# Output projections of two later mixers: squaring on ScalarE and the gain on VectorE as results leave PSUM

## The chip, the cores and the metric

The kernel runs on one core of a Trainium2 chip. A time is the device time of one execution in microseconds (us). The core has TensorE (matmul, with its weight load shown apart as PEld), VectorE (DVE), ScalarE (ACT), GpSimd (POOL) and SyncE (SP, which issues the transfers here). They run unsynchronized and wait for each other on semaphores. The profiler records one execution, with the clock granted to TensorE: 1.0 is 2.4 GHz, 0.5 is 1.2 GHz.

## The reference, cut to what matters

The model is a first block (a mixer and a mixture of experts) and then two layers, one "even" and one "odd". In float32, for 512 tokens of width 1024:

```python
for layer in range(2):
    nw = norm_w[layer]
    f = swiglu(rmsnorm(h, nw[0]), ...)
    h = h + 0.5 * rmsnorm(f, nw[1])
    u = rmsnorm(h, nw[2])
    m = even_mixer(u, ...) if layer % 2 == 0 else odd_mixer(u, ...)   # ends in o @ w_out
    h = h + rmsnorm(m, nw[3])
    f = swiglu(rmsnorm(h, nw[4]), ...)
    h = h + 0.5 * rmsnorm(f, nw[5])
```

`rmsnorm(m, g)` is `m / sqrt(mean(m*m) + eps) * g`, over the 1024 columns of a token. The case is about `m = o @ w_out`, `h + rmsnorm(m, nw[3])`, and the next `rmsnorm(h, nw[4])`, of each of the two layers. `w_out` has 1024 rows in the even layer and 2048 in the odd one.

## The kernel before

Tokens lie on partitions in `NT` = 4 tiles of 128. `x` (in the profile `x_tokens`) holds h for all of them. A float32 matrix is multiplied as two parts, a high one rounded to the matmul's format and a low one, the rest. `product` (L446 to L450) issues three matmuls: high by high, high by low and low by high. ScalarE writes the high part of a weight (L775, L779), VectorE the low part (L808, L812), both from a raw buffer (`weight_pieces`) that SyncE fills.

The kernel is a sequence of stages. A stage (`Stage`, `block`) gives each engine its own list of instructions in written order; nothing is reordered. At its end is a barrier: the next stage's first instructions (L55 is a jump of it) start when all engines are through. Semaphore waits inside a stage tie the lists together.

**The projection** (`project`, L569) walks over the columns of `w_out` in 4 chunks of 256 (`CHUNK_COLS`). For each chunk, TensorE forms 4 units, one for each tile of tokens, each in a PSUM bank of its own (banks 0 to 3), with 3 x 8 matmuls in the even layer and 3 x 16 in the odd one. Split weights have two buffers, the raw ones one. In `run`, ScalarE and VectorE first split chunk c+1 and then evict the units of chunk c: ScalarE copies units 1 and 3 (L746), VectorE units 0 and 2 (L748), to `m` (in the profile `even_m`, and `odd_y`, where the odd layer keeps m). SyncE had chunk 0 loaded in the stage before, so it only counts up `w_in` (L647), which releases ScalarE's first split; it loads chunk 1 when the first low part is through (L662), and at its end the two gain rows nw[3] and nw[4], spread over all partitions (L666). TensorE runs one filler call first (`keep_busy`, L2433: a matmul of constants, two instructions of 512 columns in the trace), then waits for the first splits and, by the counter from L753, for VectorE to be through with the last of them.

**The seam** (`add_normed`, L2862, which uses the class `Seam`) computes for each tile: ScalarE squares the tile of m and sums the squares into one column (L2492, an ACTIVATE and an ACTIVATION_READ_ACCUMULATOR), adds eps and takes the root (L2496); VectorE inverts it (L2558), forms `part` = m * inverse * gain (L2562) and adds it to x (L2567). Then ScalarE squares x (L2501), takes the root (L2503), VectorE inverts it (L2572), GpSimd forms x * next gain (L2634), and ScalarE (even tiles, L2509) or VectorE (odd tiles, L2578) multiplies by the inverse. TensorE turns the tile by 8 transposes (L2471), ScalarE writes the high part (L2513), VectorE the low part (L2582). Ahead of each tile's transposes stand two filler calls, and three behind the last tile. SyncE loads the first pieces of the next stage's weights meanwhile (L456). That next stage is the feed-forward part (`ffn_products`), which starts with one filler call and the splits of its first weights (L2801, L2846).

## Time and profile before

| | us |
|---|---|
| Three runs, median (lowest to highest) | 3506.04 (3501.19 to 3513.92) |
| The profiled execution, its own time | 3513.73 |
| Its span, first to last instruction | 3511.9 |
| Even projection, from TensorE's first filler to its last matmul | 1814.53 to 1862.98 |
| Even seam, to TensorE's last filler | 1862.98 to 1889.91 |
| Odd projection, likewise | 3021.57 to 3115.00 |
| Odd seam, likewise | 3115.00 to 3141.93 |

Times inside the span are counted from its start. In a timeline, a row gives start, length, engine, line, operation, output and inputs, the count of merged instructions, and in square brackets the idle time of that engine ahead of it with what ended it. Lengths of instructions in a row overlap a little, so the next start tells more than the sum of lengths. In a row of windows come the length of the stretch, then each engine's busy time and count, the granted clock, the share of DMA time and GB/s.

### The profile page before, as it was taken

To read this page: it belongs to the slowest core of one execution; us is meant where nothing else is said; L and a number is where in the kernel's file an instruction comes from. 1 tells how busy PE (TensorE), PEld (TensorE's weight loads), DVE (VectorE), ACT (ScalarE), POOL (GpSimd) and SP (SyncE) were. 2 spreads that over 40 slices of the span, in tenths; PEclk is the share of its full clock that TensorE was granted. 3 is DMA by queue.
4 is the path that set the end of the run, shared out by engine and by line. 5 is a ranking of instruction groups with operands and counts; after the bars stand their busy time and mean duration, and the time that the engine had idled before them with its cause. 6 is when DMAs were issued, how large, how long until landed. Compare 5 with 4: busy or idle time off the path is not lost. (4 is left out here: it accounts for less than half of the span.)

```text
span 3511.9 us, 45082 instructions
## 1 busy us (share of the span) xinstructions
PE 3126.3 (89%) x18490; PEld 2408.1 (69%) x18490; DVE 1266.8 (36%) x1501; ACT 990.7 (28%) x1456; POOL 356.5 (10%) x230
## 2 busy tenths in 40 slices
PE   6997658877758999998778999999999989789999
PEld 4985643322327888786776888788888865778887
DVE  3237651111123332335344332333222448443322
ACT  3116410000013221334223222322224444432222
POOL 2980000000000000100101000100000007110000
PEclk8999879999879999998889999999999999899999
DMA  6523268999973333220012332233222310313332
GB/s 226 174 87 146 64 271 358 428 427 428 428 297 84 96 98 106 72 84 16 2 57 76 97 99 100 87 96 96 96 84 84 93 53 2 108 49 96 96 99 86
DMA packets 303395, 487.06 MB, mean 139 GB/s; under 512 B 15778, under 2 KB 259965, under 8 KB 289679
## 3 DMA queue, kind: packets, MB, share of 16 engines
q1 hardware_dynamic: 298474, 467.35, 38.3%
q10 hardware_dynamic: 2468, 9.20, 0.7%
q0 software_dynamic: 2304, 8.39, 0.6%
q8 instruction: 111, 1.82, 0.2%
q14 instruction: 38, 0.30, 0.0%
HBM read 457.62 MB, written 27.28 MB: 138 GB/s over the span
## 5 line engine op out<-in xcount | busy, mean ns | idle before, releaser
L448 PE MATMUL psum_banks<-u_high,f_ffn_w_high 128*128 128x512 f32 x1408 | 549.6, 390 | 0.7 <-DVE f_ffn_w_low L2846 0.7
L449 PE MATMUL psum_banks<-u_low,f_ffn_w_high 128*128 128x512 f32 x1408 | 548.8, 390 | 0.0
L450 PE MATMUL psum_banks<-u_high,f_ffn_w_low 128*128 128x512 f32 x1408 | 548.7, 390 | 0.0
L2829 DVE TENSOR_TENSOR f_ffn_w_low<-weight_pieces,f_ffn_w_high 128x2048 fp32r<-128x2048 f32 x128 | 293.5, 2293 | 403.0 <-ACT f_ffn_w_high L2790 403.0
L2790 ACT ACTIVATE f_ffn_w_high<-weight_pieces 128x2048 fp32r<-128x2048 f32 x128 | 244.0, 1907 | 325.4 <-PE psum_banks L450 322.0
L448 PEld LDWEIGHTS psum_banks<-u_high,f_ffn_w_high 128*128 128x128 f32 x1408 | 264.8, 188 | 58.6 <-issue 3.9
L450 PEld LDWEIGHTS psum_banks<-u_high,f_ffn_w_low 128*128 128x128 f32 x1408 | 264.7, 188 | 54.9
L449 PEld LDWEIGHTS psum_banks<-u_low,f_ffn_w_high 128*128 128x128 f32 x1408 | 264.7, 188 | 54.9 <-issue 0.3
L448 PE MATMUL psum_banks<-f_ffn_w_high,f_hidden_high 128*128 128x512 f32 x704 | 275.0, 391 | 3.6 <-issue 3.6
L450 PE MATMUL psum_banks<-f_ffn_w_high,f_hidden_low 128*128 128x512 f32 x704 | 274.3, 390 | 0.0
L449 PE MATMUL psum_banks<-f_ffn_w_low,f_hidden_high 128*128 128x512 f32 x704 | 274.3, 390 | 0.0
L2022 PE MATMUL psum_banks<-expert_ring,experts_x_t 128*64 128x512 f32 x1024 | 229.1, 603 | 22.9 <-DMA expert_ring<-in_expert_w_up 21.5
L2834 DVE TENSOR_TENSOR f_ffn_whole<-f_ffn_silu,psum_banks 128x512 f32<-128x512 f32 x88 | 60.5, 688 | 468.9 <-PE psum_banks L450 468.9
L2797 ACT ACTIVATE f_hidden_high<-f_ffn_whole 128x512 f32 (+1 forms) x88 | 55.6, 632 | 502.1 <-DVE f_ffn_whole L2834 502.1
L2022 PEld LDWEIGHTS psum_banks<-expert_ring,experts_x_t 128*64 128x64 f32 x1024 | 77.1, 139 | 171.9 <-issue 170.1
L448 PEld LDWEIGHTS psum_banks<-f_ffn_w_high,f_hidden_high 128*128 128x128 f32 x704 | 132.2, 188 | 32.1 <-issue 5.2
L450 PEld LDWEIGHTS psum_banks<-f_ffn_w_high,f_hidden_low 128*128 128x128 f32 x704 | 132.2, 188 | 27.4
L449 PEld LDWEIGHTS psum_banks<-f_ffn_w_low,f_hidden_high 128*128 128x128 f32 x704 | 132.3, 188 | 27.2
L2059 PE MATMUL psum_banks<-expert_ring,experts_hidden_t 128*64 128x512 f32 x512 | 128.3, 659 | 18.5 <-DVE experts_hidden_t L2089 18.5
L2634 POOL TENSOR_TENSOR weight_pieces<-x_tokens,f_ffn_whole 128x1024 f32<-128x1024 f32 x12 | 28.7, 2392 | 1129.0 <-DVE x_tokens L2567 1129.0
L2105 ACT ACTIVATE experts_silu<-psum_banks 128x512 f32<-128x512 f32 x16 | 9.6, 597 | 455.3 <-PE psum_banks L2022 455.3
L448 PE MATMUL psum_banks<-mix_in_w_high,h_t_high 128*128 128x256 f32 x416 | 117.7, 283 | 1.5 <-DVEq L753 1.3
(654 smaller groups left out, 5587.2 us busy)
## 6 DMA issues: line engine op xcount, KB each, us to landing
expert_ring<-in_expert_w_gate SPq DMA_DIRECT2D x32, 2048.0 KB, 34.8
expert_ring<-in_expert_w_up SPq DMA_DIRECT2D x30, 2048.0 KB, 35.2
expert_ring<-in_expert_w_down SPq DMA_DIRECT2D x28, 2048.0 KB, 39.6
weight_pieces<-in_ffn_w_gate SPq DMA_DIRECT2D x88, 512.0 KB, 4.0
weight_pieces<-in_ffn_w_up SPq DMA_DIRECT2D x88, 512.0 KB, 5.3
weight_pieces<-in_ffn_w_down SPq DMA_DIRECT2D x88, 512.0 KB, 4.1
weight_pieces<-in_odd_w_in SPq DMA_DIRECT2D x20, 1024.0 KB, 5.4
mix_in_mod_w<-in_w_ada SPq DMA_DIRECT2D x32, 512.0 KB, 3.7
```

The lines of the kernel that those rows point to most:

```text
L448: nc.tensor.matmul(out, lhs.high, rhs.high, start=start, stop=False, skip_group_check=True)
L449: nc.tensor.matmul(out, lhs.high, rhs.low, start=False, stop=False, skip_group_check=True)
L450: return nc.tensor.matmul(out, lhs.low, rhs.high, start=False, stop=stop, skip_group_check=True)
L2022: last = nc.tensor.matmul(k.ps[half, bank, :], self.xt[:, q, half], self.rows_of(n, a, q * HID, HID), start=q == 0, stop=q == KD - 1)
L2059: last = nc.tensor.matmul(k.ps[half, 5 + b, :], self.ht[:, c, half], self.rows_of(n, a, c * D + b * BANK, BANK), start=c == 0, stop=c == H ...
L2105: nc.scalar.activation(self.sg[:], k.ps[:, 2, :], ACT.Silu).then_inc(self.silu_ok, 1)
L2634: nc.gpsimd.tensor_tensor(self.xn[:, t % 2, :], self.k.x[:, t, :], self.next_gain, ALU.mult).then_inc(self.xg_ok, 1)
L2790: nc.scalar.activation(w.high[:, j], raw[:, j], ACT.Copy).then_inc(w_high, 1)
L2797: nc.scalar.activation(tile_of(hidden.high, t), whole[:, j, :], ACT.Copy).then_inc(h_high, 1)
L2829: nc.vector.tensor_tensor(w.low[:, j], raw[:, j], w.high[:, j].bitcast(F32), ALU.subtract).then_inc(w_low, 1)
L2834: nc.vector.tensor_tensor(whole[:, j, :], sg[:, j, :], k.ps[:, 2 * j + 1, :], ALU.mult).then_inc(whole_ok, 1)
```

## The change

Both output projections get a new kind of part, `Gained`. ScalarE squares every unit of a chunk out of PSUM, with its sum into one column per tile and chunk; VectorE then multiplies every unit out of PSUM by the slice of the gain row nw[3] into `m`. So `m` holds m * gain, and the sums of squares of m are there when the projection ends: 4 per tile. SyncE issues the load of the row nw[3] as the stage's first transfer, ahead of the count that releases ScalarE; VectorE waits for it at its products. The row nw[4] is loaded at the end as before.

`add_normed` no longer uses `Seam`. One reduction adds the 4 sums of all tiles, one root and one reciprocal serve all of them, and one three-operand instruction per tile forms x = m * inverse + x. The squares of x stay with ScalarE; the second scaling, x * inverse * next gain, is one three-operand instruction on VectorE. GpSimd has nothing left there. TensorE waits for the first square of x, runs three filler calls, then all four tiles' transposes, then three filler calls. The even projection's padding `apart` is 128 in place of 192; with the new small buffers, its split weights start 2048 bytes further on. In the odd layer the new buffers lie in unused parts of old ones.

The diff, cut to its core:

```diff
+class Gained:
+    def __init__(self, gain, gain_row, junk, sums):
+        self.gain, self.gain_row, self.junk, self.sums = gain, gain_row, junk, sums
@@ project: SyncE
+            if measured:
+                sp.dma_start(measured.gain, measured.gain_row).then_inc(gain_in, 16)
             for part in walk:
@@ project: copies, on ScalarE and on VectorE
+                        elif part.gained:
+                            convolve(part, c, u)
@@ project: ScalarE
+            def square(c, u):
+                eng.wait_ge(mm, c * NT + (u + 2))
+                eng.wait_ge(squared, c * NT + (u + 1))
+                nc.scalar.activation(measured.junk[:, u % 2, :], k.ps[:, u, 0:CHUNK_COLS], ACT.Square, scale=D ** -0.5,
+                                     accum_out=measured.sums[:, u, bass.ds(c, 1)]).then_inc(squared, 1)
@@ project: VectorE
+            def multiply(part, c, u):
+                v.wait_ge(gain_in, 16)
+                v.wait_ge(squared, c * NT + (u + 3))
+                nc.vector.tensor_tensor(part.dest(c, part.units[u]), k.ps[:, u, 0:CHUNK_COLS],
+                                        part.gained.gain[:, bass.ds(c * CHUNK_COLS, CHUNK_COLS)], ALU.mult).then_inc(free_v, 1)
@@ add_normed: TensorE
-            seam.tensor(pe)
+            pe.wait_ge(squares, 1)
+            keep_busy(k, 0, 3)
+            for t in range(NT):
+                pe.wait_ge(xn_ok, t + 1)
+                for i in range(KD):
+                    last = nc.tensor.transpose(banks(t)[:, i, :], xn[:, t % 2, i * P:(i + 1) * P], k.c("ident"))
+                last.then_inc(turned, 1)
+            pe.wait_ge(low_ok, 1)
+            keep_busy(k, 0, 3)
@@ add_normed: ScalarE
-            seam.scalar(eng)
+            eng.wait_ge(summed, 1)
+            nc.scalar.activation(f_moments, f_moments, ACT.Sqrt, bias=eps[:, 0:1]).then_inc(f_roots, 1)
+            measure(0)
+            measure(1)
+            measure(2)
+            high(0)
+            measure(3)
+            high(1)
+            high(2)
+            high(3)
@@ add_normed: VectorE
-            seam.vector(v)
+            nc.vector.tensor_reduce(f_moments, sums, AX.X, ALU.add).then_inc(summed, 1)
+            v.wait_ge(f_roots, 1)
+            nc.vector.reciprocal(f_moments, f_moments).then_inc(f_inverse, 1)
+            v.wait_ge(f_inverse, 1)
+            def add(t):
+                nc.vector.scalar_tensor_tensor(out=x[:, t, :], in0=f[:, t, :], scalar=f_moments[:, t:t + 1], in1=x[:, t, :],
+                                               op0=ALU.mult, op1=ALU.add).then_inc(x_ok, 1)
+            def normed(t):
+                v.wait_ge(roots, t + 1)
+                nc.vector.reciprocal(moment(t), moment(t)).then_inc(inverse, 1)
+                v.wait_ge(inverse, t + 1)
+                if t >= 2:
+                    v.wait_ge(turned, t - 1)
+                nc.vector.scalar_tensor_tensor(out=xn[:, t % 2, :], in0=x[:, t, :], scalar=moment(t), in1=next_gain,
+                                               op0=ALU.mult, op1=ALU.mult).then_inc(xn_ok, 1)
@@ even_layer (odd_layer likewise)
+        project(k, "even_out", mix_t, a["even_w_out_2"][0], [
+            (0, D, token_units(NT), by_tokens(m), Gained(gains[:, 0, :], everywhere(nw[3:4]), junk, m_sums))], out_raw,
+                also=[(gains[:, 1, :], everywhere(nw[4:5]))], apart=128)
```

VectorE's order in the seam is `add` of tiles 0, 1 and 2, `normed(0)`, `add(3)`, `normed(1)`, `normed(2)`, `low(0)`, `normed(3)`, `low(1)` to `low(3)`.

VectorE in the even seam, before; `even_m` is the projection's result, `even_post_part` the scaled tile, `even_post_xn` the tile for the transposes:

```order
L2558 RECIPROCAL even_post_stats<-even_post_stats 128x1
L2562 SCALAR_TENSOR_TENSOR even_post_part<-even_m,even_post_stats,even_post_gains 128x1024
L2567 TENSOR_TENSOR x_tokens<-x_tokens,even_post_part 128x1024
L2558 RECIPROCAL even_post_stats<-even_post_stats 128x1
L2562 SCALAR_TENSOR_TENSOR even_post_part<-even_m,even_post_stats,even_post_gains 128x1024
L2572 RECIPROCAL even_post_stats<-even_post_stats 128x1
L2567 TENSOR_TENSOR x_tokens<-x_tokens,even_post_part 128x1024
L2558 RECIPROCAL even_post_stats<-even_post_stats 128x1
L2562 SCALAR_TENSOR_TENSOR even_post_part<-even_m,even_post_stats,even_post_gains 128x1024
L2572 RECIPROCAL even_post_stats<-even_post_stats 128x1
L2567 TENSOR_TENSOR x_tokens<-x_tokens,even_post_part 128x1024
L2578 TENSOR_SCALAR even_post_xn<-even_post_xn,even_post_stats 128x1024
```

VectorE in the even seam, now:

```order
L2960 TENSOR_REDUCE even_post_stats<-even_m_sums 128x4
L2962 RECIPROCAL even_post_stats<-even_post_stats 128x4
L2966 SCALAR_TENSOR_TENSOR x_tokens<-even_m,even_post_stats,x_tokens 128x1024 x3
L2971 RECIPROCAL even_post_stats<-even_post_stats 128x1
L2975 SCALAR_TENSOR_TENSOR even_post_xn<-x_tokens,even_post_stats,even_post_gains 128x1024
L2966 SCALAR_TENSOR_TENSOR x_tokens<-even_m,even_post_stats,x_tokens 128x1024
L2971 RECIPROCAL even_post_stats<-even_post_stats 128x1
L2975 SCALAR_TENSOR_TENSOR even_post_xn<-x_tokens,even_post_stats,even_post_gains 128x1024
L2971 RECIPROCAL even_post_stats<-even_post_stats 128x1
L2975 SCALAR_TENSOR_TENSOR even_post_xn<-x_tokens,even_post_stats,even_post_gains 128x1024
L2980 TENSOR_TENSOR u_low<-psum_banks,u_high 128x8x128
L2971 RECIPROCAL even_post_stats<-even_post_stats 128x1
```

Two long operations per tile (a three-operand product and an addition) became one, the reciprocals of the first norm became one, and the product with the next gain came over from GpSimd.

TensorE around the even seam, before (L2433 are filler calls, two recorded instructions each; L2471 are transposes):

```order
L2874 UNCONDITIONAL_BRANCH
L2433 MATMUL psum_banks<-const_table 128x512 x2
L2471 MATMUL psum_banks<-const_table,even_post_xn 128x128 x8
L2433 MATMUL psum_banks<-const_table 128x512 x2
L2471 MATMUL psum_banks<-const_table,even_post_xn 128x128 x8
L2433 MATMUL psum_banks<-const_table 128x512 x2
L2471 MATMUL psum_banks<-const_table,even_post_xn 128x128 x8
L2433 MATMUL psum_banks<-const_table 128x512 x2
L2471 MATMUL psum_banks<-const_table,even_post_xn 128x128 x8
L2433 MATMUL psum_banks<-const_table 128x512 x3
L55 UNCONDITIONAL_BRANCH
```

TensorE there, now (L2466 are the filler calls, L2928 the transposes, L2744 the next stage):

```order
L55 UNCONDITIONAL_BRANCH
L2921 UNCONDITIONAL_BRANCH
L2466 MATMUL psum_banks<-const_table 128x512 x3
L2928 MATMUL psum_banks<-const_table,even_post_xn 128x128 x32
L2466 MATMUL psum_banks<-const_table 128x512 x3
L55 UNCONDITIONAL_BRANCH
L2744 UNCONDITIONAL_BRANCH
L2466 MATMUL psum_banks<-const_table 128x512
```

The fillers between the tiles are gone; three calls stand ahead of all transposes and three behind them.

## Rows read from the trace of the kernel before

**Rows 1.** The page: busy time, share of the span and instructions of each engine.

```profile
PE 3126.3 (89%) x18490; PEld 2408.1 (69%) x18490; DVE 1266.8 (36%) x1501; ACT 990.7 (28%) x1456; POOL 356.5 (10%) x230
```

**Rows 2.** Timeline, TensorE, even seam: start us, us, engine line, op, count, idle before.

```profile
1866.83 3.39 PE L2433 MATMUL psum_banks<-const_table 128*128 128x512 f32 x4 [3.85 <-DVE even_post_part L2562]
...
1886.25 1.09 PE L2471 MATMUL psum_banks<-const_table,even_post_xn 128*128 128x128 f32 x8 [0.52 <-DVE even_post_xn L2578]
...
1887.17 2.74 PE L2433 MATMUL psum_banks<-const_table 128*128 128x512 f32 x6
```

**Rows 3.** The same, odd seam.

```profile
3118.84 3.68 PE L2433 MATMUL psum_banks<-const_table 128*128 128x512 f32 x4 [3.84 <-DVE odd_post_part L2562]
...
3139.19 2.74 PE L2433 MATMUL psum_banks<-const_table 128*128 128x512 f32 x6
```

**Rows 4.** Timeline, ScalarE, even seam.

```profile
1863.02 0.38 ACT L746 ACTIVATE even_m<-psum_banks 128x256 f32<-128x256 f32 x1 [5.27 <-PE psum_banks L450]
...
1863.68 0.20 ACT L2486 ACTIVATE even_post_stats<-const_table 128x1 f32<-128x1 f32 x1 [0.29 <-PEq L55]
...
1864.96 0.29 ACT L2496 ACTIVATE even_post_stats<-even_post_stats,const_table 128x1 f32<-128x1 f32 x1
...
1868.06 1.06 ACT L2501 ACTIVATE even_post_junk<-x_tokens 128x1024 f32<-128x1024 f32 x1 [1.45 <-DVE x_tokens L2567]
...
1869.03 0.19 ACT L2501 ACTIVATION_READ_ACCUMULATOR even_post_junk<-x_tokens 128x1 f32 x1
...
1879.00 1.00 ACT L2513 ACTIVATE u_high<-psum_banks 128x1024 fp32r<-128x1024 f32 x1
```

**Rows 5.** Timeline, VectorE, even seam.

```profile
1865.48 1.28 DVE L2562 SCALAR_TENSOR_TENSOR even_post_part<-even_m,even_post_stats,even_post_gains 128x1024 f32<-128x1024 f32 x1
...
1868.14 3.41 DVE L2562 SCALAR_TENSOR_TENSOR even_post_part<-even_m,even_post_stats,even_post_gains 128x1024 f32<-128x1024 f32 x1
...
1888.43 1.23 DVE L2582 TENSOR_TENSOR u_low<-psum_banks,u_high 128x1024 fp32r<-128x1024 f32 x1 [1.11 <-ACT u_high L2513]
```

**Rows 6.** Timeline, GpSimd, even seam.

```profile
1868.11 2.36 POOL L2634 TENSOR_TENSOR even_post_xn<-x_tokens,even_post_gains 128x1024 f32<-128x1024 f32 x1 [117.45 <-DVE x_tokens L2567]
```

**Rows 7.** Transfers issued at L666: ns min/median/max, then landing of all of them.

```profile
L666 SPq DMA_DIRECT2D even_post_gains<-in_norm_w x2: 418/421/424, 1837.8 to 1838.3; - x2
...
DMA to landing us min/median/max: 4.1/5.9/9.0
```

**Rows 8.** Timeline, start of the even projection and its first chunks, three engines.

```profile
1814.36 2.19 ACT L775 ACTIVATE even_out_w_high<-weight_pieces 128x512 fp32r<-128x512 f32 x4 [1.03 <-SPq L647]
...
1814.53 2.04 PE L2433 MATMUL psum_banks<-const_table 128*128 128x512 f32 x2 [3.84 <-PEq L55]
...
1816.67 0.58 PE L448 MATMUL psum_banks<-even_out_w_high,even_mix_t_high 128*128 128x256 f32 x1
...
1824.89 2.29 DVE L812 TENSOR_TENSOR even_out_w_low<-weight_pieces,even_out_w_high 128x2048 fp32r<-128x2048 f32 x1 [7.37 <-ACT even_out_w_high L779]
...
1829.10 0.38 ACT L746 ACTIVATE even_m<-psum_banks 128x256 f32<-128x256 f32 x1 [3.97 <-PE psum_banks L450]
...
1837.58 0.42 DVE L748 COPY even_m<-psum_banks 128x256 f32<-128x256 f32 x1 [0.18 <-PE psum_banks L450]
```

**Rows 9.** Windows: length, busy us and counts (PE, PEld, DVE, ACT, POOL), clock, DMA.

```profile
1816.60:1818.30 1.70, 1.63 (x7) 1.63 (x8) 0.92 (x2) 0.00 (x0) 0.00 (x0) 0.50 0.01 5
...
1818.60:1862.90 44.30, 44.30 (x377) 44.17 (x376) 9.91 (x11) 8.32 (x10) 0.00 (x0) 1.00 0.29 96
...
3025.40:3030.00 4.60, 4.58 (x21) 4.58 (x22) 1.73 (x2) 0.00 (x0) 0.00 (x0) 0.50 0.35 100
...
3030.50:3114.90 84.40, 84.40 (x746) 84.30 (x744) 16.31 (x11) 13.37 (x10) 0.00 (x0) 1.00 0.24 80
...
3127.40:3132.60 5.20, 5.18 (x13) 3.01 (x14) 5.16 (x6) 3.66 (x7) 2.81 (x1) 0.50 0.00 0
...
1890.00:1900.00 10.00, 9.40 (x39) 7.22 (x40) 4.79 (x5) 5.88 (x7) 0.00 (x0) 1.00 0.58 149
```

77 lines of the change are left out of this document (60 added, 17 removed).

## The prediction

> **What bounds the kernel now.** The page comes first: TensorE is busy for 89% of the span, VectorE for 36%, ScalarE for 28% [rows 1]. So work on the other engines counts only where TensorE stands idle for it. The next view is TensorE in order of time around the two places that the diff touches. While an output projection runs, its matmuls are back to back and the evictions lie beside them. The stage behind it (from here the seam) is different: from 1862.98 (the first filler's start 1866.83, less the 3.85 us idle ahead of it), where the last projection matmul ends, to 1889.91 (1887.17 + 2.74), where the last filler ends, TensorE runs 32 short transposes and some fillers and waits for the other engines [rows 2]. That is 26.93 us. The odd seam has nearly the same length: 3115.00 (3118.84 - 3.84) to 3141.93 [rows 3]. These two stretches, 54 us of 3512, are all that the change can shorten. Everything behind them is TensorE's own work, so a gain there is kept.
>
> Then the engines inside the even seam. ScalarE squares each tile of the projection's result before VectorE may scale it; the first scaled product starts at 1865.48 [rows 5]. VectorE then runs for each tile a three-operand product and an addition. The first product takes 1.28 us, the second 3.41 [rows 5]. The second starts at 1868.14, GpSimd's product of the same stage at 1868.11, and GpSimd's lasts until 1870.47 [rows 6]; 1.08 us later VectorE's ends. GpSimd has four such products, and VectorE three long ones beside them. I read the 2.1 us of excess as waiting for GpSimd.
>
> The Trainium skill ("SBUF — State Buffer", section "SBUF: two separate sides") says that a VectorE instruction with two SBUF inputs and a GpSimd one that reads SBUF take a shared port pair in turns, whole instruction by whole instruction. By that rule every product costs 1.28 us once GpSimd is out of the seam; were it wrong, the sum would be that of the fourth case below. The trace agrees, with the 1.08 us just named.
>
> **Step 1, the projection.** ScalarE now squares all four results of a chunk and VectorE multiplies all four, where each copied two. Two more squares (0.38 us as the copy [rows 4], and 0.19 us to read the accumulator, as behind the square of x) and two more products (0.42 us as the copy [rows 8]) lie beside 11.3 us of matmuls per chunk. What TensorE needs from VectorE is the low half of the next weights: for chunk 1 it ends at 1827.18 (1824.89 + 2.29), and the last result of chunk 0 is evicted only at 1829.10 [rows 8], so 1.9 us are to spare. I cost the loop at nothing; without that cover it would be 1 us per chunk. The gain row's transfer, 512 KB, is issued first. Its wait stands at VectorE's first product, some 13 us later, with the three other products and the next low half queued behind it, and TensorE behind those. The row's landing has no exact match: transfers issued at the same line landed after 4.1 to 9.0 us [rows 7]. It is hidden.
>
> What is not hidden is its issue. ScalarE's first weight split is released by SyncE [rows 8], which must now issue the row first: 0.42 us, the median of the even gains' two issues [rows 7]. TensorE's start hangs on that split, so 0.42 us are lost per projection. In the even one a second loss is possible: the filler ended at 1816.57 and the first matmul followed at 1816.67 [rows 8]; now 0.5 us are idle between them. The granted clock stood at 0.50 until 1818.3, 1.7 us after that start, and at 1.00 behind it. In the odd one, with 1.8 us idle there, it stood at 0.50 for 4.6 us after the start [rows 9]. If the longer pause sets the clock's rise back likewise, 2.9 us more run at half clock, 1.4 us lost. Between 0 and 1.4 I take 0.5, since a pause of 0.5 lies nearer to the short one.
>
> **Step 2, the tail.** Before, the last copy ended 0.42 us after the last matmul and ScalarE's next stage began at 0.70 [rows 4]. Now the last result goes through square, accumulator and product in a row: 0.38 + 0.19 + 0.42, with hops about 1.0; plus the same 0.28 for the barrier gives 1.3.
>
> **Step 3, the first row sum.** Gone are four squares of the result and the long products with the gain. In their place is one reduction over 128x16, for which no row stands: between a 128x1 operation of 0.16 and a copy of 256 columns of 0.42, I take 0.2, nearer to the small one. From the start of the square root to the scaled product was 0.52 (1864.96 to 1865.48 [rows 4, 5]). So the first addition begins at 1.3 + 0.2 + 0.05 + 0.52, about 2.05 after the last matmul, and ends at 3.35 (1.28, as above). The square of x with its accumulator takes 1.16 (1868.06 to 1869.22 [rows 4]): at **4.6** TensorE may begin its fillers.
>
> **Step 4, the fillers.** Three calls make six instructions, ahead of all transposes. TensorE is at the lower of its two clock levels (1.2 GHz) then: after 3.8 us idle, the four filler instructions of before took 3.39 us, and 3.68 in the odd seam [rows 2, 3]. At full clock (2.4 GHz) six take 2.74 [rows 2], so four 1.8. Six at the low level are 3.68 x 6/4, at most 5.5. In the even seam the clock rose before the fourth ended (3.39 is less than 3.68), some 3 us after the start; in the odd one it stayed at 0.50 through 5.2 us of work from 3127.4 on [rows 9]. With the rise at 3 us, 3.3 instructions are done and 2.7 at 0.46 are left: 4.3. So 4.3 to 5.5; I take 4.9, the middle. The first transposes can begin at **9.5**. The scaled row is ready by 7.2, so these fillers are what is late.
>
> **Step 5, the rest.** From there in a chain: transposes of tile 0, 1.05; their high half 1.0; the square of tile 3, which ScalarE runs behind it, with its root 1.5; reciprocal and hop 0.3; product 1.28; transposes 1.1; fillers 2.74 at full clock: 8.9, less small overlaps **8.8**. VectorE's last low half ends within 0.3 us of that. The seam becomes 18.3 us (17.7 to 18.8).
>
> **The sum.** 26.9 - 18.3 - 0.42 = 8.2 us per seam, 16.4 for both, less 0.5: 15.9. The profiled execution took 3513.73 us (span 3511.9 and 1.8 around it); it becomes 3497.8. The median of the runs shown is 7.7 lower, 3506.04, with 12.7 between the ends of the three, so I forecast **3490**.
>
> **Rivals.**
> 1. *The clock falls before the seam ends.* TensorE idles 1.6 us ahead of the last transposes. If that is enough, the last six fillers take 5.5 instead of 2.74: 2.7 per seam, 3495.4. For: the projection's start in step 1. Against: once at full clock it stayed there over a pause of 0.52 us ahead of the old seam's last transposes [rows 2], and at 1.00 from 1890 to 1900, with 0.6 us idle [rows 9]. Neither is as long as 1.6.
> 2. *The clock is still full at the fillers.* Then six take 2.74 and each seam is 2.2 shorter: 3485.7. Against it speak the slow fillers after a shorter pause, 3.8 us [rows 2, 3].
> 3. *A hidden loss in the projection.* The gain row's packets delay chunk 1's weights, or the moved weight buffers change the spacing of matmuls. The even projection's recorded matmuls are 44.30 / 377 = 0.1175 us apart, the odd one's 84.40 / 746 = 0.1131, 4% less [rows 9]; 4% of both projections' 139 us is 5.6. With little for the weights: some 6 us, 3496.
> 4. *The three-operand products stay slow by themselves.* This one ends slower. The new seam has eight of them on VectorE in a row. If 3.3 us is their price when operands lie so, GpSimd or not, VectorE needs 2.05 + 8 x 3.3 + four low halves of 1.23 + reciprocals 0.8 = 34.2 us, 7.7 more per seam than 26.9 with the late start, 3521. It decides from 2.4 us per product. Against: the first, with GpSimd idle, took 1.28 [rows 5].
> 5. *The row is late.* VectorE stands at its first product, and TensorE at chunk 1. That costs only beyond about 15 us after issue; the longest landing was 9.0 [rows 7].
>
> **Chances.** Forecast within 3 us: 0.62. Rival 1: 0.14. Rival 2: 0.08. Rival 3: 0.10. Rival 4: 0.03, rival 5: 0.01; 0.02 is for something else. A measurement of this kernel tells about 0.3%, 10.5 us, from no change. Forecast, rival 2 and a half of rivals 1 and 3 are beyond it, 0.82; the other halves are within, 0.13; with rivals 4 and 5 and the medians' own spread slower has 0.05. The range takes in rivals 1 to 3 and a few us for the medians: 3481 to 3500.
>
> **What would show it.** The seam from last projection matmul to last filler: 17.7 to 18.8 us. Three-operand products at 1.28, GpSimd empty there. Fillers starting 4.6 after the last matmul and lasting 4.3 to 5.5. The first projection matmul 0.4 later against the stage's start. TensorE's spacing within the projection unchanged. I am wrong if the fillers don't delay the transposes, if VectorE's products exceed 1.3, or if TensorE waits inside the projection.

## The result

| | us |
|---|---|
| The changed kernel, five runs, median (lowest to highest) | 3488.13 (3486.49 to 3489.62) |
| The kernel before, five runs beside it | 3506.33 (3501.19 to 3513.92) |
| Ratio, with its 95% interval | 0.9946 (0.9936 to 0.9957) |
| The profiled execution of the changed kernel | 3489.62, span 3487.8 |
| Even seam / odd seam (before: 26.93 each) | 18.41 / 18.84 |
| First filler of the projection to the next stage's filler, even / odd | 67.02 / 112.72 (before: 75.83 / 120.81) |

The median fell by 18.2 us, 0.52%, and 3490 had been forecast. Here are the rows of the changed kernel that answer to those of before. First the page's line of the engines; against [rows 1], GpSimd has 8 instructions and 19 us less, the four products of either seam.

```profile
PE 3117.5 (89%) x18470; PEld 2398.9 (69%) x18470; DVE 1256.5 (36%) x1509; ACT 984.8 (28%) x1478; POOL 337.5 (10%) x222
```

The timeline of TensorE, even seam, then odd, answers to [rows 2, 3]. The last projection matmul ends at 1857.46 (1862.09 - 4.63) and at 3099.01.

```profile
1862.09 5.24 PE L2466 MATMUL psum_banks<-const_table 128*128 128x512 f32 x6 [4.63 <-ACT even_post_junk L2941]
1867.16 1.91 PE L2928 MATMUL psum_banks<-const_table,even_post_xn 128*128 128x128 f32 x16
...
1872.19 1.09 PE L2928 MATMUL psum_banks<-const_table,even_post_xn 128*128 128x128 f32 x8 [1.45 <-DVE even_post_xn L2975]
1873.12 2.74 PE L2466 MATMUL psum_banks<-const_table 128*128 128x512 f32 x6
...
3103.62 5.49 PE L2466 MATMUL psum_banks<-const_table 128*128 128x512 f32 x6 [4.61 <-ACT odd_post_junk L2941]
...
3115.11 2.74 PE L2466 MATMUL psum_banks<-const_table 128*128 128x512 f32 x6
```

ScalarE and then VectorE in the even seam, answering to [rows 4, 5]: the last result is squared (L799) and multiplied (L851) in a row, the barrier lies between 1858.4 and 1858.8, the three additions (L2966) are one merged row of 3.68 us, and the scaled rows (L2975) take 1.28 each. VectorE stands still once, for 1.01 us, for transposes of TensorE.

```profile
1857.49 0.38 ACT L799 ACTIVATE even_m_junk<-psum_banks 128x256 f32<-128x256 f32 x1 [2.25 <-PE psum_banks L450]
...
1858.79 0.20 ACT L2935 ACTIVATE even_post_stats<-const_table 128x1 f32<-128x1 f32 x1 [0.83 <-PEq L55]
1860.88 1.06 ACT L2941 ACTIVATE even_post_junk<-x_tokens 128x1024 f32<-128x1024 f32 x1 [1.56 <-DVE x_tokens L2966]
```

```profile
1858.06 0.42 DVE L851 TENSOR_TENSOR even_m<-psum_banks,even_post_gains 128x256 f32<-128x256 f32 x1 [2.30 <-ACT even_m_junk L799]
1858.82 0.17 DVE L2960 TENSOR_REDUCE even_post_stats<-even_m_sums 128x4 f32<-128x16 f32 x1 [0.33 <-PEq L55]
1859.57 3.68 DVE L2966 SCALAR_TENSOR_TENSOR x_tokens<-even_m,even_post_stats,x_tokens 128x1024 f32<-128x1024 f32 x3
1863.35 1.28 DVE L2975 SCALAR_TENSOR_TENSOR even_post_xn<-x_tokens,even_post_stats,even_post_gains 128x1024 f32<-128x1024 f32 x1
...
1868.31 1.28 DVE L2975 SCALAR_TENSOR_TENSOR even_post_xn<-x_tokens,even_post_stats,even_post_gains 128x1024 f32<-128x1024 f32 x1 [1.01 <-PE psum_banks L2928]
...
1872.06 3.55 DVE L2980 TENSOR_TENSOR u_low<-psum_banks,u_high 128x1024 fp32r<-128x1024 f32 x3
```

The start of the even projection, answering to [rows 8]: SyncE issues the row (L655), ScalarE's first split has waited 1.43 us where it was 1.03, and TensorE pauses 0.49 us between filler and first matmul where it was 0.1. While chunk 0 is evicted, VectorE's low half of chunk 1 ends at 1822.34 and its last product at 1825.85; TensorE has no wait there.

```profile
1809.09 0.35 SPq L655 DMA_DIRECT2D even_post_gains<-in_norm_w  x1
```

```profile
1809.52 0.63 ACT L790 ACTIVATE even_out_w_high<-weight_pieces 128x512 fp32r<-128x512 f32 x1 [1.43 <-SPq L660]
```

```profile
1809.29 2.05 PE L2466 MATMUL psum_banks<-const_table 128*128 128x512 f32 x2 [3.83 <-PEq L55]
1811.83 0.58 PE L448 MATMUL psum_banks<-even_out_w_high,even_mix_t_high 128*128 128x256 f32 x1 [0.49 <-DVEq L768]
```

```profile
1820.05 2.29 DVE L837 TENSOR_TENSOR even_out_w_low<-weight_pieces,even_out_w_high 128x2048 fp32r<-128x2048 f32 x1 [7.37 <-ACT even_out_w_high L794]
...
1825.43 0.42 DVE L851 TENSOR_TENSOR even_m<-psum_banks,even_post_gains 128x256 f32<-128x256 f32 x1 [2.09 <-ACT even_m_junk L799]
```

Windows, with the columns of [rows 9]: the even seam's fillers and what follows, the odd seam's fillers, and both projections at full clock. The matmuls come 39.40 / 349 = 0.1129 us apart in the even projection (0.1175 before) and 82.90 / 733 = 0.1131 in the odd (as before). A window also counts matmuls that its ends cut, so these quotients are slightly small, in all traces alike: from start to start it is 0.1134 in both projections here.

```profile
1862.10:1867.30 5.20, 5.20 (x8) 2.21 (x9) 5.13 (x7) 2.93 (x7) 0.00 (x0) 0.53 1.17 279
1867.30:1876.00 8.70, 6.54 (x39) 4.27 (x37) 7.26 (x7) 5.20 (x7) 0.00 (x0) 1.00 0.00 1
3103.50:3108.50 5.00, 4.88 (x6) 2.08 (x7) 4.93 (x7) 3.02 (x8) 0.00 (x0) 0.50 1.20 292
...
3016.00:3098.90 82.90, 82.90 (x733) 82.81 (x731) 19.18 (x18) 17.57 (x33) 0.00 (x0) 1.00 0.22 71
1818.00:1857.40 39.40, 39.40 (x349) 39.25 (x347) 12.67 (x18) 12.42 (x33) 0.00 (x0) 1.00 0.20 67
```

The two stretches from a projection's first filler to the next stage's filler give 8.81 + 8.09 = 16.9 us. The two profiled spans differ by 24.1. The other 7 us lie in stages that the change doesn't touch, most of them in two: from the first to the last matmul on `mix_in_w`, the first block's input weights, it took 182.5 us before and 178.7 now, and on `odd_in_w`, the odd layer's, 239.7 and 236.9. From the lists of before and of after, the first of three kinds of the former, its matmuls shorter in the mean:

```profile
L448 PE MATMUL psum_banks<-mix_in_w_high,h_t_high 128*128 128x256 f32 x416 | 117.7, 283 | 1.5 <-DVEq L753 1.3
```

```profile
L448 PE MATMUL psum_banks<-mix_in_w_high,h_t_high 128*128 128x256 f32 x416 | 116.1, 279 | 1.7 <-DVEq L768 1.4 <-DVE tok L763 0.2
```

So two profiled runs cannot be subtracted to a few us; the argument below goes by the stretches and the medians.

### The profile page after: what moved, and what is told of

Same layout as the page of the kernel before. It is cut to its first block and busy times, and to the rows that moved or that the text cites. A ratio compares the mean times of both kernels' runs of the same rounds, so it can differ in the third digit from the quotient of the medians.

```text
span 3487.8 us, 45099 instructions
## 1 busy us (share of the span) xinstructions
PE 3117.5 (89%) x18470; PEld 2398.9 (69%) x18470; DVE 1256.5 (36%) x1509; ACT 984.8 (28%) x1478; POOL 337.5 (10%) x222
## 5 line engine op out<-in xcount | busy, mean ns | idle before, releaser
L2092 PE MATMUL psum_banks<-expert_ring,experts_hidden_t 128*64 128x512 f32 x512 | 137.4, 698 | 17.7 <-DVE experts_hidden_t L2122 17.7
```

The costliest lines, as they stand in the source:

```text
L2092: last = nc.tensor.matmul(k.ps[half, 5 + b, :], self.ht[:, c, half], self.rows_of(n, a, c * D + b * BANK, BANK), start=c == 0, stop=c == H ...
```

## Experiments

All against the changed kernel. "Seam" is, as in the prediction, last projection matmul to end of the last filler. "Both stretches" is the sum of the two stretches just named (before: 196.6). The ratios are each to the kernel before on the same chip.

| kernel | median us (runs) | ratio, 95% interval | seam even / odd | both stretches |
|---|---|---|---|---|
| changed kernel | 3488.13 (5) | 0.9946 (0.9936 to 0.9957) | 18.41 / 18.84 | 179.7 |
| e1, row later | 3488.59 (4) | 0.9951 (0.9935 to 0.9968) | 17.71 / 18.89 | 177.5 |
| e2, no first fillers | 3487.92 (4) | 0.9945 (0.9929 to 0.9962) | 17.42 / 17.57 | 181.2 |
| e3, early fillers | 3487.21 (4) | 0.9950 (0.9933 to 0.9967) | 17.41 / 17.40 | 177.0 |
| e4, GpSimd beside | 3505.52 (1) | | 25.84 / 26.59 | 197.0 |
| e5, projection undone | 3499.97 (10) | 0.9979 (0.9969 to 0.9988) | 23.44 / 25.76 | 190.2 |
| e6, GpSimd's product back | 3505.33 (1) | | 24.68 / 25.78 | 192.5 |
| e7, e1 and e3 together | 3490.39 (4) | 0.9957 (0.9942 to 0.9973) | 17.41 / 19.08 | 179.9 |
| e8, fused | 3482.22 (5) | 0.9931 (0.9918 to 0.9945) | 13.69 / 14.28 | 178.6 |
| e9, fused, kept busy | 3487.65 (5) | 0.9949 (0.9935 to 0.9962) | 12.71 / 12.40 | 173.6 |
| e10, changed kernel again | 3490.13 (5) | 0.9956 (0.9943 to 0.9970) | 18.18 / 18.88 | 182.4 |
| e11, e9 with weights in place | 3480.32 (5) | 0.9925 (0.9911 to 0.9938) | 12.86 / 12.39 | 170.9 |
| e12, weights 64 bytes on | 3496.89 (8) | 0.9972 (0.9961 to 0.9982) | 18.68 / 17.70 | 185.7 |

### Is it GpSimd? (e4, e5, e6)

e4 adds GpSimd's products where they had been; nothing reads them.

```diff
+        @block.gpsimd
+        def _(pool):
+            for t in range(NT):
+                pool.wait_ge(x_ok, t + 1)
...
+                nc.gpsimd.tensor_tensor(beside[:], x[:, t, :], next_gain, ALU.mult).then_inc(beside_ok, 1)
```

> Edit of the changed kernel: GpSimd forms x * next gain into a buffer of its own that nobody reads, behind each of the four additions of a seam, as extra work. Theory (a VectorE product with two SBUF inputs and a GpSimd one take turns): of the eight three-operand products of a seam, those that meet one of the four GpSimd products take 3.3 us instead of 1.28, at least three of them; tile 0's scaled copy is ready at 11 to 13.5 us behind the last matmul instead of 7.2, and the seam grows by 3 to 6 us from 18.4. Rival (the 3.4 us of before came from the operands' place or the PSUM traffic of the time): all eight stay at 1.28, the seam at 18.4.

The seams grew by 7.4 and 7.7 us, more than expected and nearly all that the change had gained. VectorE's timeline, then GpSimd's, in the even seam: the three additions take 5.83 instead of 3.68 and the next products 3.24 to 3.45, while GpSimd works. Once it is through, at 1876.8, they are back at 1.28.

```profile
1861.76 5.83 DVE L2967 SCALAR_TENSOR_TENSOR x_tokens<-even_m,even_post_stats,x_tokens 128x1024 f32<-128x1024 f32 x3
1867.69 3.24 DVE L2976 SCALAR_TENSOR_TENSOR even_post_xn<-x_tokens,even_post_stats,even_post_gains 128x1024 f32<-128x1024 f32 x1
1870.86 3.43 DVE L2967 SCALAR_TENSOR_TENSOR x_tokens<-even_m,even_post_stats,x_tokens 128x1024 f32<-128x1024 f32 x1
1874.40 3.45 DVE L2976 SCALAR_TENSOR_TENSOR even_post_xn<-x_tokens,even_post_stats,even_post_gains 128x1024 f32<-128x1024 f32 x1
1877.95 1.28 DVE L2976 SCALAR_TENSOR_TENSOR even_post_xn<-x_tokens,even_post_stats,even_post_gains 128x1024 f32<-128x1024 f32 x1
```

```profile
1863.12 10.08 POOL L3002 TENSOR_TENSOR even_post_beside<-x_tokens,even_post_gains 128x1024 f32<-128x1024 f32 x3 [117.49 <-DVE x_tokens L2967]
1874.37 2.40 POOL L3002 TENSOR_TENSOR even_post_beside<-x_tokens,even_post_gains 128x1024 f32<-128x1024 f32 x1 [1.17 <-DVE x_tokens L2967]
```

Both engines pay: three of GpSimd's products take 10.08 us together, 3.4 each. The last starts 0.03 us ahead of VectorE's at 1874.40, takes 2.40, and VectorE ends 1.08 us behind it. The same instructions at the same lines cost 1.28 or 3.4 by what GpSimd does. So a price of their own (rival 4) is out.

e5 does the other half: GpSimd stays out, and the projections store as before, so that the norm of the result is back in the seam.

```diff
-            (0, D, token_units(NT), by_tokens(m), Gained(gains[:, 0, :], everywhere(nw[3:4]), junk, m_sums))], out_raw,
+        project(k, "even_out", mix_t, a["even_w_out_2"][0], [(0, D, token_units(NT), by_tokens(m))], out_raw,
...
+                nc.vector.scalar_tensor_tensor(out=part[:], in0=f[:, t, :], scalar=mom, in1=gain,
+                                               op0=ALU.mult, op1=ALU.mult).then_inc(product_ok, 1)
+                v.wait_ge(product_ok, t + 1)
+                nc.vector.tensor_tensor(x[:, t, :], x[:, t, :], part[:], ALU.add).then_inc(x_ok, 1)
```

> The projections store their results as the kernel before does (plain copies by both engines, no gain, no squares), and the seam does the whole of the branch's norm; GpSimd has no work in it. Per tile ScalarE squares the result, VectorE forms result times inverse times gain (1.28 us), adds it (about 1.2) and forms the scaled row (1.28). Theory (GpSimd's presence is most of the price, the moved work the rest): VectorE's row is twelve operations of 1.2 to 1.3 and four subtractions of 1.17, 19.5 us with the reciprocals, behind a start of 2.5 to 3 and with a wait or two: seam 22.5 to 24, so of the 8.5 us per seam between 26.9 and 18.4 some 4 belong to GpSimd and some 4.5 to the moved products; total 8 to 11 us above the changed kernel, and no row issue at the projection's start (first matmul 0.4 us earlier). Rival A (the moved work is all that counts, VectorE's operations are as long as before): seam near 27. Rival B (GpSimd's presence is all that counts): seam below 20.

The even seam, 23.44, lies in the expected 22.5 to 24. VectorE's product starts 2.51 us after the last matmul (1855.87), at 1.28, the addition at 1.22. The odd one, 25.76, doesn't: there TensorE's clock fell before the end, seen in its timeline by transposes of 1.97 and six fillers of 4.23 in place of 1.09 and 2.74. VectorE itself was through at 3126.56, 24.06 after the last matmul.

```profile
1858.38 1.28 DVE L2973 SCALAR_TENSOR_TENSOR even_post_part<-even_m,even_post_stats,even_post_gains 128x1024 f32<-128x1024 f32 x1
```

```profile
3122.27 1.97 PE L2928 MATMUL psum_banks<-const_table,odd_post_xn 128*128 128x128 f32 x8 [0.95 <-DVE odd_post_xn L2984]
3124.03 4.23 PE L2466 MATMUL psum_banks<-const_table 128*128 128x512 f32 x6
```

e6 keeps the projections of the changed kernel and gives GpSimd the product x * next gain again; VectorE only applies the inverse.

```diff
-                nc.vector.scalar_tensor_tensor(out=xn[:, t % 2, :], in0=x[:, t, :], scalar=moment(t), in1=next_gain,
-                                               op0=ALU.mult, op1=ALU.mult).then_inc(xn_ok, 1)
+                v.wait_ge(xg_ok, t + 1)
+                nc.vector.tensor_scalar(xn[:, t % 2, :], xn[:, t % 2, :], moment(t), None, ALU.mult).then_inc(xn_ok, 1)
...
+                nc.gpsimd.tensor_tensor(xn[:, t % 2, :], x[:, t, :], next_gain, ALU.mult).then_inc(xg_ok, 1)
```

> The changed kernel's projections and its fused addition stay; only the scaled row is split again as in the kernel before: GpSimd forms x times the next gain (about 2.4 us), VectorE applies the inverse to the product (an operation with one tensor operand). Theory (every three-operand product of VectorE beside a GpSimd product is late by about 2 us): the additions of tiles 1 to 3 run beside GpSimd's and take 3.2 to 3.5 each instead of 1.28, the operations with one tensor operand stay below 1 us; seam 20 to 23 us against 18.4, total 4 to 9 us above the changed kernel. Rival (GpSimd's product is harmless where its reader is not behind it, VectorE even saves 0.5 us per tile by the shorter operation): seam 16.5 to 18.5.

24.68 and 25.78, above even the theory's 20 to 23. The missing part is in VectorE's rows: the scaling with one tensor operand, which I had put below 1 us, took 2.65 and 2.91 beside GpSimd, and 0.75 alone. Another 1.76 us is a wait of VectorE for GpSimd's fourth product, which my own wait for a free buffer had held back.

```profile
1861.95 5.77 DVE L2967 SCALAR_TENSOR_TENSOR x_tokens<-even_m,even_post_stats,x_tokens 128x1024 f32<-128x1024 f32 x3
1867.84 2.65 DVE L2975 TENSOR_SCALAR even_post_xn<-even_post_xn,even_post_stats 128x1024 f32<-128x1024 f32 x1
...
1871.79 2.91 DVE L2975 TENSOR_SCALAR even_post_xn<-even_post_xn,even_post_stats 128x1024 f32<-128x1024 f32 x1
...
1874.81 0.75 DVE L2975 TENSOR_SCALAR even_post_xn<-even_post_xn,even_post_stats 128x1024 f32<-128x1024 f32 x1
```

The Trainium skill ("SBUF — State Buffer", section "SBUF: two separate sides") names two kinds of VectorE instruction that lock out GpSimd and are locked out by it: those with two SBUF inputs, and those in a two-port performance mode. The 0.75 us alone and 2.65 beside GpSimd agree with the second kind; that this operation runs in such a mode is my reading, since no row tells the mode.

What follows from the three: in the even seam, taking GpSimd out without the move gives 26.93 - 23.44 = 3.5 us, moving the products into the projection with GpSimd's product left in 26.93 - 24.68 = 2.3, and both 8.5. These are not pure shares: e5 and e6 also have the new order of TensorE, without fillers between the tiles, and e6 has the wait of 1.76 us just named, which the kernel before has not. The two halves help each other: the move leaves VectorE with operations in an unbroken row, and each one that a GpSimd product meets is late. In the whole, e5 is 12 us above the changed kernel's median, and e4 and e6, a single run each, 17; for e6, 4 to 9 had been expected.

### What comes behind the fillers? (e2, e3)

e2 takes the three filler calls ahead of the transposes out.

```diff
-            pe.wait_ge(squares, 1)
-            keep_busy(k, 0, 3)
```

> Edit of the changed kernel: the three filler calls ahead of the seam's first transposes are left out. Theory (they hold the transposes back, 9.7 us behind the last matmul where the scaled tile is ready at 7.2, but they also raise the clock for what follows): transposes of tile 0 start at 7.2 and take 1.9 at half clock, the six filler instructions at the end take 5.5 instead of 2.74, and the seam comes out at 19 to 21 us, against 18.4; the total is 1 to 5 us above the changed kernel's. Rival (the clock is not worth its fillers, since the transposes are few): the seam is 15.8 to 17 us and the total 3 to 5 us below.

e3 starts six of them at once instead.

```diff
-            pe.wait_ge(squares, 1)
-            keep_busy(k, 0, 3)
+            keep_busy(k, 0, 6)
```

> Edit of the changed kernel: six filler calls (twelve instructions) run at once from the seam's start, without a wait for the first square of x, in place of three behind that square. Theory (a pause of 1.3 us leaves the clock at its full level, as the 1.45 us ahead of the last transposes did): fillers from 1.3 to 6.8 us behind the last matmul, at full clock, transposes of tile 0 at 7.2 instead of 9.7, seam 15.9 us; 2.5 us per seam and 5 in all below the changed kernel. Rival (the clock falls in the pause at the barrier): twelve instructions at 0.9 us end at 12.2, the seam is 21 us and the total 5 us above.

Both seams end at 17.4 to 17.6, 1.0 to 1.4 below the changed kernel's, by opposite ways. None of the four lengths that had been expected came true (19 to 21 or 15.8 to 17 for e2, 15.9 or 21 for e3), and the medians differ by less than the runs spread. Without fillers (first fence) the transposes of tile 0 run at the lower level, 1.97 us, but start 7.24 us after the last matmul. With early ones (second fence) TensorE pauses only 1.36 us, keeps full clock over it, and the transposes start at 7.23. In both, VectorE's row decides.

```profile
1863.13 1.97 PE L2926 MATMUL psum_banks<-const_table,even_post_xn 128*128 128x128 f32 x8 [7.24 <-DVE even_post_xn L2973]
```

```profile
1856.44 5.39 PE L2466 MATMUL psum_banks<-const_table 128*128 128x512 f32 x12 [1.36 <-PEq L55]
1862.32 1.09 PE L2927 MATMUL psum_banks<-const_table,even_post_xn 128*128 128x128 f32 x8 [0.49 <-DVE even_post_xn L2974]
```

In e3's odd seam the clock did fall for a while: behind a pause of 1.50 us the transposes of tiles 1 and 2 took 3.36 us together, with the granted clock at 0.50 from 3104.3 to 3106.5. The last transposes were back at 1.09, and the seam lost nothing by it.

```profile
3103.01 3.36 PE L2927 MATMUL psum_banks<-const_table,odd_post_xn 128*128 128x128 f32 x16 [1.50 <-DVE odd_post_xn L2974]
```

From its first addition (2.11 us after the last matmul) VectorE has 8 operations at 1.2 start to start, 4 low parts at 1.15 and 4 reciprocals at 0.19 without a break: 2.1 + 9.6 + 4.6 + 0.8 = 17.1. That is the seam's second bound, 1.3 behind the first. It was named in the prediction ("within 0.3 us of that") but as an end that coincides, not as what remains when the fillers go.

### The start of the projection (e1, e7)

e1 issues the row behind the first weights' count.

```diff
             for part in walk:
...
                 if loaded and not part.chunks:
                     sp.sem_inc(w_in, 16)
...
+                if measured:
+                    sp.dma_start(measured.gain, measured.gain_row).then_inc(gain_in, 16)
```

> Edit of the changed kernel: SyncE first counts up for ScalarE's first weight split and then issues the gain row's transfer. Theory (the issue stands on the path to TensorE's start, and the longer pause behind the first filler sets the clock's rise back in the even projection): from filler start to first matmul 2.14 us in the even projection (now 2.54) and 3.85 in the odd (now 4.22), and half clock for 1.7 us behind the even start instead of 3.9; 1.8 us less in all, all of it ahead of the seams, which stay at 18.4 and 18.8. Rival (the slow start has another cause than the pause): only 0.4 per projection comes back, 0.8 in all, and half clock lasts 3.9 us as before. Second rival (VectorE now waits for the row): TensorE has a pause at chunk 1.

```profile
1811.90 2.04 PE L2466 MATMUL psum_banks<-const_table 128*128 128x512 f32 x2 [3.84 <-PEq L55]
1814.11 0.58 PE L448 MATMUL psum_banks<-even_out_w_high,even_mix_t_high 128*128 128x256 f32 x1 [0.17 <-DVEq L768]
```

From filler to first matmul 2.21 us instead of 2.54 in the even projection, 3.92 instead of 4.22 in the odd; the issue costs 0.3, once for each. The clock rose 4.0 us after the filler's start, as before the change (4.0), against 6.5 in the changed kernel. (The even seam of 17.71 is no doing of the edit: its first six fillers took 4.54 us, where the same six took 5.24 in the changed kernel's profile, 5.02 in e10 and 5.49 in e12.) Over all traces of this study the even projections with a pause of 0.46 to 0.50 us rose after 5.6 to 7.6 us (eight traces, mean 6.4), those with 0.1 to 0.34 after 3.8 to 6.6 (six traces: 3.8, 4.0, 4.0, 4.3, 6.0, 6.6, mean 4.8). So the longer pause goes with 1.6 us more at half clock on average, 0.8 us of work; single runs of the two groups overlap. The odd projections show no such thing: there the clock rose 8.0 to 8.8 us after the filler's start with 1.8 or 1.9 us of pause (four traces) and 7.7 to 8.9 with 2.2 to 3.1 (ten traces). The total, 3488.59, can't show so little.

e7 is e1 and e3 together.

> Both small gains together: the gain's row issued behind the first weights' count, and the seam's first fillers not waiting for the first tile's squares (six of them at once). Theory: the projection's first matmul 0.3 us and the rise of the clock 2.5 us earlier in the even one (about 1.3 us of work), seam 17.4 instead of 18.4 and 18.8: 1.3 to 2.5 us per segment, 3 to 5 us in total, median 3483 to 3486. Rival (VectorE takes all of it back): within 1.5 us of the changed kernel.

The forecast of 3483 to 3486 was wrong: 3490.39. The even seam came out as said, 17.41, but the even projection's clock rose 5.9 us after the filler's start, not about 4. In the odd seam the clock fell before the last transposes, after a pause of 1.43 us, the same pause over which it held in the changed kernel (1.46) and in e3's even seam (1.43). TensorE, odd seam:

```profile
3109.82 1.94 PE L2927 MATMUL psum_banks<-const_table,odd_post_xn 128*128 128x128 f32 x8 [1.43 <-DVE odd_post_xn L2974]
3111.55 3.62 PE L2466 MATMUL psum_banks<-const_table 128*128 128x512 f32 x6
```

That is rival 1 of the prediction, at 1.7 us (19.08 less 17.40) in place of 2.7. The clock also fell inside the seam in e3 (odd seam, above), in e5 (odd seam), and in both seams of e4, e6 and e8, there behind pauses of 2.2 us and more, and in none of the four seams of the changed kernel's two profiles. The 1.7 us explain only a part of the miss: the profiled execution, with the fallen clock in it, took 3486.97, and the other three 3487.14 to 3495.96. Why the median lies higher is open.

### A shorter row for VectorE (e8, e9)

Since VectorE's row is the bound, e8 takes out of the seam what can be done while TensorE works on the last chunk: tiles 0 to 2 are summed, inverted and added as soon as their last 256 columns are out, x's squares taken for tiles 0 and 1, and the scaled row of tile 0 formed.

```diff
+                    if part.gained:
+                        for u in range(U):
+                            convolve(part, c + 1, u)
+                            finish(part, c + 1, u)
...
+            def finish(part, c, u):
...
+                nc.vector.tensor_reduce(f, g.sums[:, u, :], AX.X, ALU.add).then_inc(t_summed, 1)
...
+                nc.vector.scalar_tensor_tensor(out=k.x[:, u, :], in0=part.dest(slice(None), part.units[u]), scalar=f, in1=k.x[:, u, :],
+                                               op0=ALU.mult, op1=ALU.add).then_inc(t_added, 1)
```

> Most of the seam moves into the projection's last chunk: as soon as a token tile's last 256 columns are out, VectorE sums that tile's squares, takes the reciprocal and adds the tile into x (tiles 0 to 2), ScalarE takes the mean squares of x for tiles 0 and 1, and VectorE forms the scaled row of tile 0, all while TensorE works on the later tiles (2.9 us each in the even projection, 5.6 in the odd). The seam has left: tile 3's sum and addition, scaled rows 1 to 3, transposes, high and low parts; the first transposes start at once. Theory (VectorE's unbroken row sets the seam's end, e3): VectorE has four three-operand operations less, 2.1 + 4 x 1.28 + 4 x 1.17 + reciprocals 0.6 = 12.5, seam 12.5 to 14 us against 17.4 to 18.8; in the even projection VectorE's row (8.8 us of work against 8.7 of TensorE's) may push the end by up to 1. Total 8 to 12 us below the changed kernel, 3476 to 3480. Rival A (the last chunk's VectorE and ScalarE work delays TensorE's banks or the last copies): projection's last chunk 1 to 4 us longer, gain half. Rival B (TensorE pauses long enough between the projection and the transposes for its clock to fall): seam 14 to 17.

Seams of 13.69 and 14.28. The median is 5.9 us below the changed kernel's, where 8 to 12 had been expected. The VectorE work is hidden: in the odd projection's last chunk VectorE still stands idle 3.42 us ahead of unit 2.

```profile
3102.26 0.42 DVE L875 TENSOR_TENSOR odd_y<-psum_banks,odd_y 128x256 f32<-128x256 f32 x1 [3.42 <-ACT odd_y L809]
```

The clock fell here before the last transposes, so e9 adds four filler calls behind tile 0's transposes and takes e1's order for the row.

```diff
+                if t == 0:
+                    keep_busy(k, 2, 4)
```

> The fused version again, with the gain's row issued behind the first weights' count, and four filler calls (eight instructions) behind tile 0's transposes, where TensorE stood 2.4 us and its last transposes took 1.97 instead of 1.09. Theory (in the fused seam the last transposes at half clock lie on the way to the last low part): transposes of tile 3 at 1.1, VectorE without its 0.85 wait, seam 13.2 to 13.6 instead of 14.1 and 14.7; with the earlier start of the projections 2 to 4 us less in total than the fused version, 10 to 12 below the changed kernel when both run on the same chip. Rival (the fillers, if the clock is at half by then, take 3.7 us and delay the transposes of tile 1): seam 14.5 to 16, no gain.

Transposes of tile 3 at 1.09, fillers at 2.74, seams of 12.71 and 12.40, better than the 13.2 to 13.6 expected. Yet the median is 3487.65, above e8's 3482.22, where 2 to 4 us less had been expected. The projections had grown: from first filler to last matmul, the odd one took 98.2 us, where it had been 93.4 before and after the change. That doesn't explain the median, for in e8 it had grown as much, to 98.7, and e9's profiled execution, with the long projections in it, took 3475.66, the shortest of the whole study. e9's five runs reach from there to 3488.57, e8's from 3480.22 to 3493.59, and the intervals of the two ratios meet. So whether e9 is better or worse than e8 in time stays open; that its seams are shorter is seen.

### The address of the weights (e10, e11, e12)

The new buffers of e8 and e9 lie ahead of the split weights and move them by 64 bytes modulo 2048 (1760 and 1312 instead of 1696 and 1248). The change itself had kept these numbers: in the even layer its two new buffers are 2048 + 64 bytes and its padding is 64 bytes smaller, and in the odd layer nothing moved. e10 is the changed kernel once more, e11 is e9 with the padding 64 bytes smaller, and e12 the changed kernel with the padding 64 bytes larger. The edit of e12 (that of e11 is the same with 64 and 128):

```diff
-                also=[(gains[:, 1, :], everywhere(nw[4:5]))], apart=128)
+                also=[(gains[:, 1, :], everywhere(nw[4:5]))], apart=192)
...
-                also=[(post[:, 1, :], everywhere(nw[4:5]))], apart=192)
+                also=[(post[:, 1, :], everywhere(nw[4:5]))], apart=256)
```

> The changed kernel itself, unaltered, beside the fused version on one chip. Theory: the rate of TensorE's multiplications inside the stages (0.113 or about 0.118 us apart, seen for the same program in different runs) belongs to the run, so the profile of this one may show either, in stages that the change doesn't touch as well; seams again 18.3 to 18.9; ratio to the kernel before 0.994 to 0.996. Rival (the spacing comes from where the program's buffers lie): every run of this program has the same spacing in the even projection as its first profile, 0.113 to 0.114.

> The fused version with fillers and later row (e9) in which the padding ahead of the split weights is 64 bytes smaller in both projections, so that the weights lie again where they lie in the changed kernel modulo 2048 bytes (offsets 1696 and 1248, while the two fused versions had 1760 and 1312). Theory (the weights' address sets how far apart TensorE's multiplications come: 0.1195 us in the odd projection of both fused versions against 0.1129 in most others): first to last multiplication 93 to 94 us becomes 88.5 to 90 in the odd projection (at worst the 92 that the changed kernel's second profile had), 46.6 becomes 45 to 46 in the even; 4 to 6 us less than the fused versions' traces, median 3479 to 3483. Rival (the spacing belongs to the run, or to the VectorE and ScalarE work that the fused version puts into the last chunk): odd stays at 93 to 94, median 3484 to 3488.

> The changed kernel with the padding ahead of the split weights 64 bytes larger in both projections (offsets 1760 and 1312 modulo 2048 instead of 1696 and 1248), everything else as in the changed kernel. Theory (the address sets the spacing): odd projection 93 to 94 us from first to last multiplication instead of 88.7 (and 92 in its second profile), even 46.5 to 48 instead of 45; total 3 to 7 us above the changed kernel, 3491 to 3496. Rival (the spacing belongs to the run or to the fused work): odd 88.7 to 92, total 3487 to 3491.

Windows of both projections at full clock, odd then even, in e10, e11 and e12, and of e9's even one:

```profile
3016.00:3099.40 83.40, 83.40 (x709) 83.22 (x707) 19.29 (x18) 17.54 (x33) 0.00 (x0) 1.00 0.18 58
1818.00:1854.90 36.90, 36.90 (x327) 36.76 (x325) 12.54 (x18) 10.40 (x32) 0.00 (x0) 1.00 0.21 72
```

```profile
3012.00:3095.90 83.90, 83.90 (x715) 83.90 (x714) 25.09 (x29) 21.09 (x42) 0.00 (x0) 1.00 0.18 60
1818.00:1857.70 39.70, 39.70 (x352) 39.70 (x351) 17.23 (x29) 15.85 (x42) 0.00 (x0) 1.00 0.20 67
```

```profile
3016.00:3102.80 86.80, 86.80 (x725) 86.69 (x723) 19.29 (x18) 17.55 (x33) 0.00 (x0) 1.00 0.19 64
1819.00:1858.80 39.80, 39.80 (x333) 39.69 (x331) 12.70 (x18) 10.81 (x33) 0.00 (x0) 1.00 0.20 67
```

```profile
1808.00:1851.00 43.00, 43.00 (x361) 43.00 (x360) 17.06 (x28) 15.69 (x41) 0.00 (x0) 1.00 0.23 76
```

Matmul to matmul: e12 0.1197 odd and 0.1195 even; e11 0.1173 and 0.1128; e10 0.1176 and 0.1128; the changed kernel's first profile 0.1131 and 0.1129; e9's even projection 0.1191. From start to start, over all fourteen traces of this study, the six projections with the weights 64 bytes on (e8, e9, e12) have 0.120, and the other 22 either 0.113 (16 of them) or 0.118 (6). So two things add. The address is one, and it accounts for every case of the highest level. It cost e12 some 8 us in the median (3496.89; its interval of the ratio, 0.9961 to 0.9982, lies above the changed kernel's 0.9936 to 0.9957; e10's, up to 0.9970, reaches into it, but each of e12's eight runs is slower than each of the ten runs of the changed kernel, though on another chip). Giving the 64 bytes back is less clear in time: e11's median is 7.3 us below e9's, on another chip, but the intervals just meet, e8 with the moved weights is only 1.9 above e11, and the two stretches show 2.7 of the 7.3. The other thing is the run: at the old address the same program had 0.1131 in one run and 0.1176 in another in its odd projection, and the kernel before had the higher one in its even projection. Both theories that were set against each other in e10 and e12 hold in part. By the two stretches alone e12 should be 3.3 to 6.0 us slower (185.7 less 182.4 or 179.7); where the rest of its 7 to 9 us lies, was not settled.

e11 has the lowest median of the study: 3480.32, ratio 0.9925 (0.9911 to 0.9938), about 8 us below the changed kernel's 3488.13 and 10 below e10's 3490.13. VectorE's shorter row and TensorE's end together again: VectorE's last low part ends at 1870.31, TensorE's last filler at 1870.57. Which of the two would bound the next step was not tried.

```profile
1867.83 2.74 PE L2510 MATMUL psum_banks<-const_table 128*128 128x512 f32 x6
```

## Why the prediction was right

**Step 1, the loop at nothing.** Right. Chunk 1's low half ended at 1822.34, three products of 1.08 us in all ran behind it and the fourth ended at 1825.85, and TensorE had no wait in either projection. The row landed 3.8 us after its issue, hidden as said.

**Step 1, the issue.** 0.42 was forecast for each projection; ScalarE's first split waited 0.40 longer, the first matmul came 0.40 later against the filler in the even projection and 0.37 in the odd, and e1 won back 0.33 and 0.30.

**Step 1, the clock.** Too small. Of 0 to 1.4 I took 0.5, because the new pause of 0.5 seemed nearer to 0.1 than to 1.8. The clock rose 6.5 us after the filler's start instead of 4.0: 1.25 us in this run, 0.8 in the mean of the traces. The term of the sum was short by 0.3 to 0.75; the mechanism behind it fits the mean of the even projections, but single traces don't follow it (e7 and e11, with 0.16 us of pause, rose at 5.9 and 6.6), and the odd ones don't at all. That the term was short didn't show, and that was luck: the even projection's matmuls ran at 0.1129 instead of 0.1175 in this run, 384 of them gave back 1.8 us, and the stretch from filler to last matmul took 48.16 instead of 48.45.

**Steps 2 and 3.** Forecast: ScalarE's next stage at 1.3, first addition at 2.05, fillers from 4.6. Measured: 1.33, 2.11 and 4.63 (odd 4.61).

**Step 4, the fillers.** Forecast 4.9 in 4.3 to 5.5; from first filler to first transposes it took 5.07 and 5.28, with the granted clock at 0.53 and 0.50. The transposes started at 9.70 and 9.89, not 9.5. They do delay them: the scaled row was ready at 7.2, as forecast. But "these fillers are what is late" was half the truth; e3 took the whole delay away and won 1.0 and 1.4 us, not 2.5.

**Step 5, the rest.** Forecast 8.8; measured 8.70 and 8.95.

**The sum.** Seams of 18.41 and 18.84 against 18.3; 16.9 us in both stretches against 15.9. The profiled execution was forecast at 3497.8 and took 3489.62, since 7 us came from stages without a change. The median, forecast at 3490 by taking 7.7 off for the runs' spread, was 3488.13. What the working stands for is the 15.9 us of the two stretches; that the number fits to 1.9 us, less than the 3.1 us by which the changed kernel's own five runs differ, is in part chance.

**Rivals.** 1, the clock before the seam's end: not here, but in e4, e5, e6, e7 and e8, so the margin is thin. 2, full clock at the fillers: no. 3, the spacing of matmuls: not through the change, which kept the weights' place modulo 2048 bytes, but real: 64 bytes would have cost a third to half of the gain. 4, slow by themselves: refuted by e4. 5, the row late: no.

## What to carry to other kernels

Where VectorE is busy with operations on two SBUF tensors, a product given to GpSimd beside it is no help: it cost VectorE 2 us at each meeting and took back 7.4 to 7.7 of the 8 us that a seam had gained. Move such work into the cover of a long TensorE stage instead, one tile at a time. And when a buffer is added, look at where the ones behind it have moved: take the spacing of matmuls from a window before and after, in more than one profile, since 64 bytes here were worth more than a third of the change, and a run by itself moved the spacing by two thirds as much (0.113 to 0.118, against 0.120 by the address).
